# Input stage of a hybrid attention block: two running q sums, and partial sums that ScalarE puts back into PSUM

## What is computed

```python
ada = c @ w_ada[l] + b_ada[l]
shift, scale, gate = jnp.split(ada, 3, axis=-1)
h = rms_norm(x, g_pre[l]) * (1.0 + scale[:, None]) + shift[:, None]
proj = h @ w_in[l]
(q_mla, c_kv, k_rope, q_diff, k_diff, v_diff,
 gate_mla, gate_diff, mg_mla, mg_diff) = jnp.split(proj, split_points, axis=-1)
```

## Time and profile before

| | |
|---|---|
| median of 3 runs | 785.51 us (785.29 to 791.23) |
| profiled execution | 788.58 us, its span 786.9 us |
| TensorE busy | 761.8 us (97%), 3569 matmuls |
| VectorE busy | 556.2 us (71%) |
| ScalarE busy | 398.1 us (51%) |
| GpSimd busy | 26.1 us (3%) |
| DMA | 189.69 MB, mean 241 GB/s |
| input stage on TensorE | piece 0 starts at 27.80 us, the first matmul behind piece 70 at 236.31 us |

### The profile page before, as it was taken

How to read it: one execution, slowest core, us unless ns; L and a number is a source line. 1 busy time by engine, 2 the same in 40 slices (tenths; PEclk the granted TensorE clock), 3 DMA queues, 4 the chain that set the end, 5 groups by cost and what they waited for, 6 DMA issues and landing times.

```text
span 786.9 us, 9831 instructions
## 1 busy us (share of the span) xinstructions
PE 761.8 (97%) x3569; PEld 627.7 (80%) x3569; DVE 556.2 (71%) x811; ACT 398.1 (51%) x627; POOL 26.1 (3%) x97
## 2 busy tenths in 40 slices
PE   5889999999999999999999999999999999999996
PEld 5767888777888888888887888888888888888884
DVE  4789999798776878887775777677546546465554
ACT  4466546536566665454554646565444444444441
POOL 2000000000000000000000010111100000000000
PEclk9799999999999999999999999999999999999999
DMA  9999999999665597888874656556665666567642
GB/s 341 391 341 376 342 333 349 321 323 341 195 202 149 199 335 260 276 280 256 294 253 144 207 173 207 165 158 180 176 192 185 178 206 192 182 222 231 224 159 107
DMA packets 118089, 189.69 MB, mean 241 GB/s; under 512 B 10197, under 2 KB 43418, under 8 KB 117786
## 3 DMA queue, kind: packets, MB, share of 16 engines
q1 hardware_dynamic: 117920, 189.04, 73.9%
q10 hardware_dynamic: 122, 0.04, 0.0%
HBM read 185.90 MB, written 2.10 MB: 239 GB/s over the span
## 4 chain that ended last, share of the span: by engine, by line
PE 86%; DVE 7%; issue 2%; ACT 2%; DMA 2%; ACTq 0%; DVEq 0%; POOLq 0%; POOL 0%
PE ps L1675 26%; PE ps L1679 25%; PE ps L1676 25%; DVE w_both L1375 2%; DVE ada_acc L1143 2%; PE ps L1611 1%; DMA w_raw<-in_w_in 1%; PE ps L1516 1%; PE ps L1492 1%; PE ps L1431 1%; DMA vec_rows<-in_g_subln 1%; PE ps L1501 1%; PE ps L1531 1%; PE ps L1505 1%; PE ps L1552 0%
## 5 line engine op out<-in xcount | busy, mean ns | idle before, releaser
L1375 DVE TENSOR_TENSOR w_both<-w_raw,w_both 128x1024 fp32r<-128x1024 f32 x248 | 301.2, 1222 | 162.3 <-ACT w_both L899 161.7
L899 ACT CAST w_both<-w_raw 128x1024 fp32r<-128x1024 f32 x248 | 259.4, 1050 | 279.3 <-PE ps L1679 214.3
L1675 PE MATMUL ps<-w_both,h_hi 128*128 128x512 f32 x700 | 280.7, 401 | 4.7 <-DVE w_both L1375 4.2
L1679 PE MATMUL ps<-w_both,h_lo 128*128 128x512 f32 x700 | 273.2, 390 | 0.0
L1676 PE MATMUL ps<-w_both,h_hi 128*128 128x512 f32 x700 | 272.8, 390 | 0.0
L1675 PEld LDWEIGHTS ps<-w_both,h_hi 128*128 128x128 f32 x700 | 131.5, 188 | 38.6 <-issue 7.8
L1679 PEld LDWEIGHTS ps<-w_both,h_lo 128*128 128x128 f32 x700 | 131.4, 188 | 28.3
L1676 PEld LDWEIGHTS ps<-w_both,h_hi 128*128 128x128 f32 x700 | 131.6, 188 | 26.9 <-issue 1.0
L1143 DVE SCALAR_TENSOR_TENSOR ada_acc<-ada_ring,cols,ada_acc 128x512 f32<-128x512 f32 x98 | 69.3, 744 | 0.5
L1675 PE MATMUL ps<-w_both,o_hi 128*128 128x512 f32 x128 | 50.6, 395 | 0.0
L1679 PE MATMUL ps<-w_both,o_lo 128*128 128x512 f32 x128 | 49.9, 390 | 0.0
(11 more groups left out here) (238 smaller groups left out, 633.2 us busy)
## 6 DMA issues: line engine op xcount, KB each, us to landing
w_raw<-in_w_in SPq DMA_DIRECT2D x177, 512.0 KB, 4.7
ada_ring<-in_w_ada SPq DMA_DIRECT2D x128, 256.0 KB, 6.5
gate_ring<-in_w_ada SPq DMA_DIRECT2D x32, 512.0 KB, 4.4
w_raw<-in_w_out SPq DMA_DIRECT2D x32, 512.0 KB, 3.9
w_raw<-in_w_o_mla SPq DMA_DIRECT2D x16, 512.0 KB, 3.6
w_raw<-in_w_o_diff SPq DMA_DIRECT2D x16, 512.0 KB, 4.1
w_raw<-in_w_ukv SPq DMA_DIRECT2D x8, 512.0 KB, 4.6
x_tok<-in_x SPq DMA_DIRECT2D x2, 1024.0 KB, 6.0
```

Source lines behind the costliest of these rows:

```text
L899: act.copy(w_hi[:, p % RING, :], w_raw[:, p % RING, :]).then_inc(hi_done, 1)
L1375: dve.tensor_tensor(w_lo[:, p % RING, :], w_raw[:, p % RING, :], w_hi[:, p % RING, :].bitcast(F32), ALU.subtract).then_inc(lo_done, 1)
L1675: mm(o, lhsT=s_hi[:, k, q], rhs=hi, start=first and r == 0, stop=False)
L1679: ins = mm(o, lhsT=s_lo[:, k, q], rhs=hi, start=False, stop=last and r == tiles - 1)
```

## The change

- Only q chunks 0 and 1 keep running sums (banks 0 to 3). q chunk 2 becomes a job done in visits, all eight pairs, with a part sum `q_part`.
- Visits alternate between banks 4, 5 and banks 6, 7 (`early_bank`). There are now 29 of them, over 55 pieces (before: 17 over 47). The stage still has 71 pieces, and the list behind it is as long as before.
- Every visit is copied out by ScalarE (`act_early`). Before a later visit of a job, ScalarE copies the part sum back into the banks (`act_seed`), and TensorE accumulates on it without a start. `add_early` is gone from VectorE. There are 29 copies out and 21 copies in (8 jobs open without one).
- A turn (`TURN`) now stands before the piece of q chunk 1 that follows the middle of the period, and goes into the bank pair of the next visit. ScalarE sums it (`sum_mod`) behind the cast of the next piece, then seeds that visit if it needs a seed. `make_h` still stands behind the cast of the second piece after the turn.
- VectorE's `ada` work and SyncE's `ada` loads stand behind `w_lo` and the load of their piece (`ada_after`), and are spread from one turn to the next. `h_lo` stands ahead of the third piece after the turn.
- Pair 0: only row tile (7, 1) is summed by TensorE, and eight matmuls of 128x128 whose result nobody reads are put in (`keep_clock`). The first piece that uses a pair of `h` (`opens`) makes its hi by hi matmuls first and waits for `w_lo` and `h_lo` only before those that need them.
- `angles` on VectorE is cut into four parts over four pieces. `POOL_PART` is empty, so GpSimd makes no `w_lo`.

```diff
 PERIODS = [
-    [(("vd", 0), (0,)), 0, (("vd", 1), (0,)), 1, (("gate", 0), (0,)), 2],
-    [(("gate", 1), (0, 1)), 0, (("gate", 2), (0, 1)), 1, 2],
...
+    [(("vd", 0), (0,)), (("vd", 1), (0,)), 0, (("gate", 0), (0,)), (("gate", 1), (0,)), (("gate", 2), (0,)), TURN, 1,
+     (("q", 2), (0,))],
+    [(("ckv", 0), (0, 1)), 0, (("gate", 3), (0, 1)), (("vd", 0), (1,)), TURN, 1, (("vd", 1), (1,))],
...
-FIRST_ON_PE = {(5, 0), (5, 1), (7, 1)}
+FIRST_ON_PE = {(7, 1)}
+POOL_PART = [()] * 8
...
-        return 6 if a is None else 2 * a if a < 3 else 2 * ((a + 1) % 2)
+        return 2 * (a % 2)
+
+    def early_bank(v):
+
+        return 4 + 2 * (v % 2)
...
-                act.copy(part_sum(VISITS[v][1]), ps[:, 6:8, :]).then_inc(early_read, 1)
+                dst = part_sum(job)
...
+                act.copy(dst, ps[:, early_bank(v):early_bank(v) + TOK, :]).then_inc(early_copied, 1)
+            return run
+
+        def act_seed(v):
+
+            def run(eng):
+                turned = [j for j in turn_at if turn_visits(j) == v]
+                wait_visit(eng, v - 2)
+                if turned:
+                    eng.wait_ge(ada_read, turned[0])
+                wait_visit(eng, max(w for w in range(v) if VISITS[w][1] == VISITS[v][1]))
+                act.copy(ps[:, early_bank(v):early_bank(v) + TOK, :], part_sum(VISITS[v][1])).then_inc(early_seeded, 1)
             return run
...
+        for v in range(len(VISITS)):
+            act_after[visit_end[v] + 2].append(act_early(v))
+            if seed_at.get(v + 2) == visit_end[v] + 2:
+                act_after[visit_end[v] + 2].append(act_seed(v + 2))
...
                 if p in h_after:
                     make_h(h_after[p])
+                if p - 1 in sum_before:
+                    sum_mod(sum_before[p - 1])
+                    if turn_visits(sum_before[p - 1]) in SEEDED:
+                        act_seed(turn_visits(sum_before[p - 1]))(eng)
...
-                dve.tensor_tensor(dst, part_sum(job), ps[:, 6:8, :], ALU.add).then_inc(early_read, 1)
...
-            pe.wait_ge(xT_copied, 3)
-            first_direct(5, True)
-            first_acc(1, ada_odd)
-            first_direct(7, False)
+            pe.wait_ge(xT_copied, 4)
+            first_acc(1, ada_odd, True)
+            keep_clock(2)
+            first_direct(7)
             first_acc(0, ada_used).then_inc(ada_turned, 1)
+            keep_clock(6)
...
-                    if n >= 1:
-                        pe.wait_ge(early_read, n)
+                    if n in SEEDED:
+                        pe.wait_ge(early_seeded, seed_order.index(n) + 1)
+                    elif n >= 2:
+                        wait_visit(pe, n - 2)
```

More of the change, by code:

```diff
@@ L133, in hybrid_block @@
         for step in period:
-            if isinstance(step, int):
+            if step == TURN:
+                sum_before[len(pieces)] = j + 1
+            elif isinstance(step, int):
                 first_part[j].append(len(pieces))
@@ L145, in hybrid_block @@
     PH1 = len(pieces)
-    acc_of = {("q", i): i for i in range(3)}
-    for a, (kind, n) in enumerate(make_jobs(), start=3):
+    acc_of = {("q", i): i for i in range(2)}
+    for a, (kind, n) in enumerate(make_jobs(), start=2):
         done = EARLY_PAIRS.get((kind, n), 0)
@@ L154, in hybrid_block @@
     NP = len(pieces)
+    POOL_LO = [first_part[j][i] for j in range(KT // 2) for i in POOL_PART[j]]
     first_piece = lambda kind, n: start[acc_of[kind, n]]
@@ L356, in hybrid_block, with wait_lo, wait_visit, wait_all_visits @@
         block = ctx.enter_context(nc.Block())
-        by_dve = [a for a in range(3, 3 + len(make_jobs())) if pieces[start[a]][1] in ("vd", "gate", "wom", "wod")]
-        by_act = [a for a in range(3 + len(make_jobs())) if a not in by_dve]
+        by_dve = [a for a in range(2, 2 + len(make_jobs())) if pieces[start[a]][1] in ("vd", "gate", "wom", "wod")]
+        by_act = [a for a in range(2 + len(make_jobs())) if a not in by_dve]
         def dve_reads(kind, n):
             return by_dve.index(acc_of[kind, n]) + 1
+        def wait_lo(eng, p):
+            if p in POOL_LO:
+                eng.wait_ge(lo_pool, POOL_LO.index(p) + 1)
+            else:
+                eng.wait_ge(lo_done, p + 1 - sum(b < p for b in POOL_LO))
+        def wait_visit(eng, v):
+            eng.wait_ge(early_copied, v + 1)
+        def wait_all_visits(eng):
+            eng.wait_ge(early_copied, len(VISITS))
         def wait_acc_read(eng, a):
@@ L766, in hybrid_block @@
         act_after[PH1 - 1].append(sin_cos)
-        for n in range(3):
+        for n in range(2):
             act_after[PH1 + n].append(act_read(n, read_q(n)))
         act_after[PH1 + 3].append(act_read(acc_of["kr", 0], read_kr))
[L770 to L776, removed]
+        act_after[visit_end[LAST_VISIT["ckv", 0]] + 4].append(square_ckv)
+        for v in range(len(VISITS)):
+            act_after[visit_end[v] + 2].append(act_early(v))
+            if seed_at.get(v + 2) == visit_end[v] + 2:
+                act_after[visit_end[v] + 2].append(act_seed(v + 2))
         act_after[last_piece("gate", 1) + 4].append(act_silu(0))
@@ L1240, in first_rows @@
                 eng.wait_ge(ada_in[q], 32)
-                for t, done, count, amount in ((1, ada_odd, q - (q > 5), 3 if q == 6 else 1),
-                                               (0, ada_used, q - (q == 6), 2 if q == 6 else 1)):
+                for t, done, amount in ((1, ada_odd, 2 if q == 6 else 1), (0, ada_used, 1)):
                     if (q, t) in FIRST_ON_PE:
@@ L1307, in angles @@
[L1307 to L1313, removed]
@@ L1314, in angles @@
-                dve.memset(gain_tmp[:, 0:1], 0.0).then_inc(angles_ready, 1)
+                if part == 0:
+                    eng.wait_ge(pos_in, 16)
+                    eng.wait_ge(consts, 3)
+                    link(eng, dve.tensor_copy(pos_qf[:, :], pos_q[:, :]))
+                    for t in range(TOK):
+                        link(eng, dve.tensor_scalar(ang[:, t * HALF:(t + 1) * HALF], freq[:, :], pos_qf[:, t:t + 1],
+                                                    None, ALU.mult))
+                    turns(k_, ang, BIG_TURN)
@@ new lines, in angles @@
+                if part == 1:
+                    less(ang, k_, BIG_PARTS[0], ang)
+                    less(ang, k_, BIG_PARTS[1], ang)
+                    link(eng, dve.tensor_scalar(r_, k_, -BIG_PARTS[2], None, ALU.mult))
+                    link(eng, dve.tensor_tensor(s_, ang, r_, ALU.add))
+                    turns(k_, s_, 2.0 * math.pi)
+                if part == 2:
+                    less(ang, k_, TURN_PARTS[0], ang)
+                    less(ang, k_, TURN_PARTS[1], ang)
+                    link(eng, dve.tensor_tensor(ang, ang, r_, ALU.add))
+                    less(ang, k_, TURN_PARTS[2], ang)
@@ L1433, in first_sum, with keep_clock, first_direct @@
                 return ins
-            def first_direct(q, first):
+            def keep_clock(count):
+                for i in range(count):
+                    mm(ps[:, 3, 0:P], lhsT=x_tok[:, 0, 0:P], rhs=x_diag[:, 0, :], start=True, stop=True)
+            def first_direct(q):
                 pe.wait_ge(ada_in[q], 32)
```

228 lines of the change are left out of this document (123 added, 105 removed).

## The result

The changed kernel takes 790.37 us (median of 20 executions) against 786.60 for the kernel before in as many. The ratio is 1.0039, with an interval of 1.0028 to 1.0049: 2.2 to 3.9 us slower, and so within 1%, as forecast. The prediction took 1% for about what a measurement can't tell from no change. The interval here is 0.1% to either side, so the 3.8 us are a real slowdown. The profiled execution took 790.24 us, its span 788.7 us.

The account below looks back on a forecast made before the run. The prediction took TensorE to bound the input stage, VectorE close behind. A start 7.4 us earlier, 2.0 us of waits gone and 12.6 us of new turn waits gave +3.1 us, 788.5 us on the median; range 775 to 797.

Parts of the forecast that it names:

- The sum: Whole input stage: piece 70 ends at 239.4 us instead of 236.3, so +3.1 us; chance as forecast 0.52.
- Term 1: Start of the input stage: piece 6 starts at 44.7 us instead of 52.1, a lead of 7.4 us.
- The first sum: Start of the stage, pair 0: ready at 23.7 us against 26.06, 2.4 us earlier, 0 to 2.4 if the clock falls.
- Load 5: Start of the stage: if landed by VectorE's 1.76 us wait, it hides two added row tiles; otherwise up to 1.5 us.
- Term 2: Input stage after 49 us: TensorE's waits for `w_lo` and small gaps go, 1.3 to 2.9 us, taken as 2.
- Term 3: Turns 2 to 7: ScalarE's added copies make TensorE wait 1.4 and 0.7 us per turn, 12.6 us in all.
- Rival 1: Turns: they cost nothing, as TensorE reaches each late anyway; 776 us; chance 0.26 together with rival 4.
- Rival 2: Whole input stage: ScalarE late throughout, held-up casts hold up loads; 10.5 us more, 799 us; chance 0.12.
- Rival 3: Start of the stage: no gain in first sum, clock falls, load 5 late; piece 6 2.4 us later, about 791; chance 0.10.
- rival 4: Turns: copies into PSUM take only 0.5 us, six turns at 0.4; about 778 us; chance 0.26 together with rival 1.

Follow-up runs that it names:

- Experiment 7: The change, but pair 1's `ada` loads and VectorE rows again ahead of pieces 1 to 4; 794.47 us, ratio 1.0093 to the kernel before.
- experiment 1: The change without the 21 copies of part sums back into PSUM (earlier part sums lost); 777.39 us, ratio 0.9874 to the kernel before.
- experiment 3: The change with the new pair of `h` made one piece later from the third turn on; 786.02 us, ratio 0.9987 to the kernel before.
- experiment 4: The change with the full value of the new `h` pair made by VectorE, not ScalarE; 788.33 us, ratio 1.0007 to the kernel before.
- experiment 8: The change without the eight `keep_clock` matmuls; 791.59 us, ratio 1.0054 to the kernel before.
- experiment 5: The change with new `h` pair later from turn 3, `h_lo` still later from turn 4, full value on VectorE; 785.52 us, ratio 0.9967 to kernel before.
- experiment 2: The change with ScalarE doing sums and next visit's copy in first, other copies behind the next cast; 796.91 us, ratio 1.0113 to the kernel before.

## Why the prediction was right

The sum gave 3.1 us more for the profiled execution; the end of the stage moved by 2.2 (236.31 to 238.49) and its time by 1.7, from 788.58 to 790.24. The medians moved by 3.8, since the profiled execution of before was itself 2 us above its median. That the prediction's +3 lies between the two is partly luck. It took the profile's sum over to the median, and the two kernels spread differently: 785.1 to 791.2 us before, 789.1 to 792.3 after. The spread of the kernel before goes with its clock: of its 34 executions that were measured beside the experiments, those of 789 us and more list 0.988 to 0.991, those below 787 us 0.992 to 0.994. Where the clock falls in the long ones no trace shows.

- **Term 1, the start.** Forecast: piece 6 at 44.7 us; it came at 44.76. Two parts erred and made each other good. The first sum was ready at 22.98 in place of 23.7. VectorE's timeline of the changed kernel:

```profile
17.47 3.58 DVE L1304 SCALAR_TENSOR_TENSOR ada_acc<-ada_ring,cols,ada_acc 128x512 f32<-128x512 f32 x5
22.98 0.16 DVE L1311 TENSOR_TENSOR mod_shift<-ps,cols 128x2 f32<-128x2 f32 x1 [1.92 <-PE ps L1490]
...
30.78 1.23 DVE L1434 TENSOR_TENSOR w_both<-w_raw,w_both 128x1024 fp32r<-128x1024 f32 x1 [0.54 <-ACT w_both L966]
...
42.03 1.54 DVE L1202 SCALAR_TENSOR_TENSOR ada_acc<-ada_ring,cols,ada_acc 128x512 f32<-128x512 f32 x2
43.49 1.22 DVE L1434 TENSOR_TENSOR w_both<-w_raw,w_both 128x1024 fp32r<-128x1024 f32 x1
```

  Load 5 had landed in the gap, as taken. But VectorE wasn't quite without idle time (0.54 and 0.17 us for casts), and its last `ada` rows end at 43.5, where 43.4 was forecast. Experiment 7 shows that this order decides 4.5 us of the lead, a clock fall of 1.7 us included.
- **Term 2, waits that go.** From piece 6 to the end of the stage it took 193.7 us; the forecast was 184.1 - 2.0 + 12.6 = 194.7. In experiment 1, without new waits, the same way took 180.3 us (43.62 to 223.89), where 184.1 - 2.0 = 182.1 was forecast. So this term was mis-sized: 3.8 us went, not 2.
- **Term 3, ScalarE's chain.** Forecast 1.4 and 0.7 us at each of six turns, 12.6 in all; measured 1.32 at each, and 0.7 (0.86 at turn 2, on the fourth piece, as forecast), 12.3 in all by these gaps. By the difference to experiment 1 (193.7 against 180.3) they cost 13.4, since the first matmuls behind a wait start further apart too (71.23 and 71.53, where 0.23 us is the rule). So terms 2 and 3 were both too small, and the errors of 1.8 and 0.8 us partly cancel. Experiments 1, 3 and 4 each take away about the part that the count gives to what they touch. The unknown price, the copy into PSUM, was taken at 1.0 us and is 1.02:

```profile
L713 ACT COPY ps<-gate_part_sum x10: 1016/1017/1018, 67.9 to 223.4; 128x1024 f32<-128x1024 f32 x10
L702 ACT COPY gate_part_sum<-ps x14: 1002/1014/1018, 37.0 to 238.7; 128x1024 f32<-128x1024 f32 x14
```

  This is the source view of the two lines (duration in ns, min/median/max). The Trainium skill (ScalarE: Activation LUTs, "Step-by-step: what each stage is for") says that ScalarE reaches PSUM sooner than SBUF as a destination. Here a 128x1024 copy from SBUF to PSUM lasts 1.017 us and one from PSUM to SBUF 1.014. These differ in their source too. The cast, which goes from SBUF to SBUF but writes another type, lasts 1.05. So the gain, if the destination makes it, is about 0.03 us in a whole copy.
- **Rival 1** (turns cost nothing) fell since TensorE reaches each of turns 2 to 7 without a wait. **Rival 2** (ScalarE late throughout, loads held up) fell: ScalarE waits 14.9 us for loads between 24 and 240 us, where it was 62.3 before. It comes to its casts later, when the loads have landed. **Rival 3** fell with piece 6 at 44.76 us, though the clock did fall at piece 0 (0.50 from 24 to 26 us), **rival 4** with the 1.02 us above.

## What to carry to other kernels

An engine at half load can still set the time if its work comes in a bunch right where the bounding engine has a short cover. Count that bunch row by row against the cover, and ask of each item whether it is wanted now. Moving an item forward helps only when the items it pushes back have a later place of their own: here one move alone cost some 6 us, and the same move on top of two others gained 5.

## What was not expected of the hardware

TensorE's clock can fall behind waits of 1.3 to 2.5 us, and need not. The same place, the first turn, shows both. The waits there are the idle times before the turn and before piece 6:

| kernel | waits, us | granted clock, 44 to 48 us |
|---|---|---|
| the change | 1.27, 0.47 | 1.00 |
| experiment 8 | 1.28, 0.47 | 0.58 |
| experiment 3 | 2.04, 0.39 | 0.61 |
| experiment 5 | 2.46, 0.41 | 1.00 |

The rows of the stretch in the change, experiment 8, experiment 3 and experiment 5, in this order, and experiment 3's row of the turn:

```profile
44.00:48.00 4.00, 3.53 (x17) 2.71 (x16) 4.00 (x7) 4.00 (x14) 0.00 (x0) 1.00 1.07 394
44.00:48.00 4.00, 3.95 (x10) 3.14 (x11) 4.00 (x6) 3.97 (x15) 0.00 (x0) 0.58 1.07 393
44.00:48.00 4.00, 3.89 (x11) 3.06 (x12) 3.69 (x7) 4.00 (x14) 0.00 (x0) 0.61 1.07 394
44.00:48.00 4.00, 3.90 (x17) 3.25 (x18) 3.70 (x7) 4.00 (x14) 0.00 (x0) 1.00 1.08 394
```

```profile
43.09 0.63 PE L1483 MATMUL ps<-ident,ada_acc 128*128 128x128 f32 x4 [2.04 <-ACT gate_part_sum L702]
```

In experiment 2 five waits of 2.4 us stand in one execution, and the clock fell behind one of them. So the length of the wait alone does not decide it here, and what does no run shows. A fall cost some 1.5 us beyond the wait: from turn 1 to turn 2 experiments 3 and 8 take 24.5 and 24.7 us, the change 23.1. A count of waits can be off by that much for each wait of this size.
